# Expert layer of a two-block transformer: 2 MB weight tiles in five slots, second gather and first sum in pieces between the passes

## The reference

```python
def swiglu(t, w_gu, w_down):
    a, g = jnp.split(t @ w_gu, 2, axis=-1)
    return (jax.nn.silu(a) * g) @ w_down

def moe_swiglu(h, w_router, w_gu, w_down):          # 8 experts, D_FF = 2816
    logits = (t @ w_router).astype(jnp.float32)
    top_logit, top_idx = lax.top_k(logits, TOP_K)   # TOP_K = 2
    top_w = jax.nn.softmax(top_logit, axis=-1)
    gate = jnp.einsum('tk,tke->te', top_w, one_hot(top_idx))
    for e in range(N_EXPERTS):
        out = out + gate[:, e:e + 1] * swiglu(t, w_gu[e], w_down[e])
```

## Time and profile before

| | us |
|---|---|
| median of 3 runs | 2047.01 (2045.9 to 2048.48) |
| the profiled execution | 2047.62 |
| its span, first to last instruction | 2045.8 |
| TensorE matmul busy | 1983.7 (97%) |
| DVE busy | 836.6 (41%) |
| ACT busy | 324.9 (16%) |
| bytes by DMA | 485.66 MB, mean 237 GB/s |

### The profile page before, as it was taken

How to read it: one execution, slowest core, us unless ns; L and a number is a source line. 1 busy time by engine, 2 the same in 40 slices (tenths; PEclk the granted TensorE clock), 3 DMA queues, 4 the chain that set the end, 5 groups by cost and what they waited for, 6 DMA issues and landing times.

```text
span 2045.8 us, 31213 instructions
## 1 busy us (share of the span) xinstructions
PE 1983.7 (97%) x13540; PEld 1253.2 (61%) x13540; DVE 836.6 (41%) x1514; ACT 324.9 (16%) x718; POOL 65.6 (3%) x72
## 2 busy tenths in 40 slices
PE   9999999999999999999999989999988999999998
PEld 4888786998458877863333333333333544855997
DVE  4555645456635466561010001110000499444446
ACT  2242111111103411210000000000000232420100
POOL 0000000000000000000000000000000035000000
PEclk9999999999999999998999999999999999999999
DMA  7533543444335244109999999899999732226240
GB/s 311 212 111 137 226 165 139 165 175 161 118 134 196 104 193 198 42 25 419 421 420 420 420 421 396 353 420 420 420 421 421 322 123 108 108 92 248 103 186 21
DMA packets 57036, 485.66 MB, mean 237 GB/s; under 512 B 6544, under 2 KB 6704, under 8 KB 9280
## 3 DMA queue, kind: packets, MB, share of 16 engines
q1 hardware_dynamic: 53424, 464.67, 56.3%
q0 software_dynamic: 3472, 18.95, 2.3%
HBM read 482.54 MB, written 1.05 MB: 236 GB/s over the span
## 4 chain that ended last, share of the span: by engine, by line
PE 87%; DMA 10%; DVE 1%; issue 1%; ACT 1%; SPq 0%; DVEq 0%; ACTq 0%
PE bank L392 46%; PE pair L392 41%; DMA weights<-in_moe_down 8%; DMA weights<-in_moe_up 2%; ACT hT L2945 0%; SPq L3475 0%; DMA const<-in_const 0%; DVE att L1869 0%; DVE h L2260 0%; DVE h L1750 0%; DVE probT L1686 0%; DVE h L1742 0%; DVE att L1870 0%; DVE big L2603 0%; ACT att L3236 0%
## 5 line engine op out<-in xcount | busy, mean ns | idle before, releaser
L392 PE MATMUL bank<-weights,att 128*32 128x512 f32 (+2 forms) x4228 | 392.6, 525 | 15.4 <-issue 13.9
L392 PEld LDWEIGHTS bank<-weights,att 128*32 128x32 f32 (+1 forms) x4228 | 145.6, 110 | 244.2 <-issue 215.3
L392 PE MATMUL pair<-weights,big 128*32 128x512 f32 (+2 forms) x1606 | 232.9, 587 | 24.2 <-DMA weights<-in_moe_down 24.2
L392 PEld LDWEIGHTS pair<-weights,big 128*32 128x32 f32 (+1 forms) x1606 | 90.3, 120 | 153.4 <-issue 149.9
L392 PE MATMUL bank<-hT,weights 128*128 128x128 f32 (+1 forms) x976 | 164.9, 325 | 0.0
L392 PEld LDWEIGHTS bank<-hT,weights 128*128 128x128 f32 x976 | 144.8, 191 | 17.2 <-issue 6.6
L2244 DVE TENSOR_TENSOR big<-head_gain,bank 128x256 f32<-128x256 f32 (+1 forms) x66 | 24.9, 377 | 295.4 <-ACT head_gain L3194 295.4
L392 PE MATMUL pair<-weights,hT 128*128 128x512 f32 (+2 forms) x336 | 137.9, 568 | 1.5 <-ACT hT L2945 1.2
L3194 ACT ACTIVATE head_gain<-bank 128x256 f32<-128x256 f32 (+1 forms) x66 | 23.0, 349 | 550.6 <-PE bank L392 550.6
L392 PEld LDWEIGHTS pair<-weights,hT 128*128 128x128 f32 x336 | 63.3, 190 | 71.5 <-issue 70.0
L392 PE MATMUL pair<-hT,weights 128*128 128x128 f32 (+1 forms) x784 | 105.0, 293 | 0.9 <-ACT hT L2945 0.8
(11 more groups left out here) (478 smaller groups left out, 2422.7 us busy)
## 6 DMA issues: line engine op xcount, KB each, us to landing
weights<-in_moe_up SPq DMA_DIRECT2D x176, 1024.0 KB, 16.7
weights<-in_moe_down SPq DMA_DIRECT2D x88, 1024.0 KB, 18.5
weights<-in_w_in SPq DMA_DIRECT2D x17, 2048.0 KB, 7.5
weights<-in_ffn_up SPq DMA_DIRECT2D x11, 2048.0 KB, 7.3
weights<-in_even_in SPq DMA_DIRECT2D x10, 2048.0 KB, 13.4
weights<-in_mem_wkv SPq DMA_DIRECT2D x8, 2048.0 KB, 7.3
weights<-in_odd_in SPq DMA_DIRECT2D x8, 2048.0 KB, 7.2
norm_par<-in_norms POOLq DMA_DIRECT2D x11, 1024.0 KB, 7.6
```

What stands on the lines that cost most here:

```text
L392: ins = pe.matmul(o, lhsT, rhs, **flags)
```

## The change

What it does, all of it in the way by few tokens:

1. Tiles are whole slots of 2 MB: for each chunk of the up part one tile of each of the four experts, for the down part steps of 4, 4, 4, 4, 4 and 2 row blocks (`FEW_DOWN`). There are 136 tiles in place of 264, five buffers in place of ten. The load of tile i waits for tile i - 5. TensorE makes each pass over the whole chunk at once. The first tile goes to slot `first + 4`, so that the stage ends with the slot ahead of the one with which the even stage begins.
2. SP reads a rank just ahead of the first tile of that expert, and in the second group just ahead of that group's tiles, in place of all eight ahead of the first load.
3. `few_gather(1)` is cut into its eight products, one behind pass 1 of each of the chunks 1 to 8 of group 0; `few_T` is doubled. `few_put(0)` is put behind pass 0 of chunk 0, `few_put(1)` behind pass 1 of chunk 10 of group 0; `put_T` is doubled.
4. `few_sum(0)` is cut into its four pieces, behind pass 1 of the chunks 1, 3, 5 and 7 of group 1. DVE's copies and additions are put in the matching places.
5. On DVE `gated_picks(0)` goes behind `few_gathered(0)`.

The core of the diff:

```diff
-            def few_half(i, first, src):
-                m = i % NHALF
-                if i >= NHALF:
-                    sp.wait_ge(*L.at(f"half{m}_used", i // NHALF))
...
+                    parts = [("moe_up", 4096 * c, 4096) for c in range(HID_CHUNKS)]
+                    parts += [("moe_down", D * sum(FEW_DOWN[:n]), D * nk) for n, nk in enumerate(FEW_DOWN)]
+                    for name, at, width in parts:
+                        for x, r in enumerate((2 * g, 2 * g + 1, 4 + 2 * g, 5 + 2 * g)):
+                            if x not in mine:
+                                mine[x] = sp.value_load(order_i[0:1, r:r + 1], min_val=0, max_val=N_EXPERTS - 1)
...
+                            s = few_slot(first, i)
+                            if taken[s]:
+                                sp.wait_ge(*L.at(f"few{s}_used", taken[s]))
...
+            def few_pass(q, steps, slots, name=None):
+                for last, j, ins in steps:
+                    if last and (q, j) in ((1, 2), (2, 1)):
+                        ins.then_inc(sems(f"few{slots[q - q % 2]}_used"), 1)
+                if name:
+                    end_late(ins, name)
+                if q and name:
+                    slot_owed[0] = f"few{slots[q - q % 2 + 1]}_used"
+                elif q:
+                    ins.then_inc(sems(f"few{slots[q - q % 2 + 1]}_used"), 1)
+
+            def few_up(g, c):
+                slots = [few_tile(), few_tile()]
+                for q in range(PASSES):
+                    if q == 2:
+                        slots += [few_tile(), few_tile()]
+                    name = ("few_up", g, c, q)
+                    o = begin(banks, name, late=True)
+                    few_pass(q, few_up_pass(g, c, q, o, slots), slots, name)
+                    if q == 0 and c:
+                        few_hidden_T(g, c - 1)
+                    if q == 0 and (g, c) == (0, 0):
+                        few_put(0)
+                    if q == 1 and g == 0 and 1 <= c <= KD:
+                        few_gather(1, c - 1)
+                    if q == 1 and (g, c) == (0, PUT_CHUNK):
+                        few_put(1)
+                    if q == 1 and g == 1 and c in SUM_CHUNKS:
+                        few_sum(0, *divmod(SUM_CHUNKS.index(c), 2))
...
                 with pe.Else():
                     few_group(0)
-                    few_gather(1)
-                    few_sum(0)
                     few_group(1)
-                    few_sum(1)
+                    for t in range(NT):
+                        for i in range(2):
+                            few_sum(1, t, i)
...
                 gates()
+                for k in range(KD):
+                    few_gathered(0, k)
                 gated_picks(0)
-                few_gathered(0)
```

More of the change, by code:

```diff
@@ L92, with few_slot, few_uses @@
 C_END = 1256
-def half_uses(m):
-    return len(range(m, FEW_TILES, NHALF))
+def few_slot(first, i):
+    return (first + FEW_FIRST + i) % NSLOT
+def few_uses(first, s):
+    return sum(few_slot(first, i) == s for i in range(FEW_TILES))
 def weight_tiles(k_tiles, widths, group):
@@ L1199, in owner, with few_up_pass @@
                 return j % 2 if q == 1 else q + j // 2
-            def few_up_pass(g, c, q, o, halves, kh):
-                for k in range(KD // 2):
+            def few_up_pass(g, c, q, o, slots):
+                for k in range(KD):
+                    if c == 0 and q == 0:
+                        pe.wait_ge(*emptied(("few_T", g, k)))
                     for j in range(4):
-                        m = halves[owner(q, j)]
-                        tile = weights[:, m // 2, HALF * (m % 2) + 512 * k:HALF * (m % 2) + 512 * k + 512]
+                        tile = weights[:, slots[owner(q, j)], 512 * k:512 * k + 512]
                         out, flow = o[QUAD * j:QUAD * j + QUAD, :], tile
@@ L1210, in few_up_pass @@
                             flow = tile.rearrange("p (a h n) -> p a h n", a=2, h=2)[:, :, j // 2, :]
[L1211 to L1215, removed]
+                        ins = mm(out, few_T[g][k][:, quad_columns(q, j)], flow, start=(k == 0), stop=(k == KD - 1))
@@ L1217, in few_down_pass @@
+                        yield k == KD - 1, j, ins
+            def few_down_pass(q, k0, nk, outs, slots):
                 for i in range(1 if q == 1 else 2):
-                    for k in range(2):
+                    for k in range(nk):
                         for j in range(4):
-                            m = halves[owner(q, j)]
-                            at = HALF * (m % 2) + D * k + 512 * (j // 2 if q == 1 else i)
+                            at = D * k + 512 * (j // 2 if q == 1 else i)
@@ L1229, in few_group @@
-            def few_group(g):
[L1230 to L1235, removed]
-                for c in range(HID_CHUNKS):
[L1237 to L1260, removed]
@@ new lines, in few_down_pass @@
+                                     weights[:, slots[owner(q, j)], at:at + 512],
+                                     start=(k0 + k == 0), stop=(k0 + k == KF - 1))
+                            yield k == nk - 1 and i == (0 if q == 1 else 1), j, ins
+            def few_pass(q, steps, slots, name=None):
[8 more added lines that the diff above has]
+                    ins.then_inc(sems(f"few{slots[q - q % 2 + 1]}_used"), 1)
@@ L1263, in few_group @@
                         [whole[2][:, i, :] for i in range(2)]]
-                for n in range(FEW_STEPS_DOWN):
-                    final = n == FEW_STEPS_DOWN - 1
+                k0 = 0
+                for n, nk in enumerate(FEW_DOWN):
+                    final = k0 + nk == KF
                     if final:
@@ L1268, in few_group @@
                             pe.wait_ge(*emptied(("few_hidT", g, HID_CHUNKS - 1, i)))
-                    halves = [half_tile(), half_tile()]
+                    slots = [few_tile(), few_tile()]
                     for q in range(PASSES):
                         if q == 2:
[L1272 to L1282, removed]
+                            slots += [few_tile(), few_tile()]
+                        few_pass(q, few_down_pass(q, k0, nk, outs[q], slots), slots, ("few_down", g, q) if final else None)
@@ L1283, in few_group @@
                     if n == 0:
                         few_hidden_T(g, HID_CHUNKS - 1)
[L1286 to L1298, removed]
+                    k0 += nk
@@ new lines, in few_sum @@
+            def few_sum(g, t, i):
+                if (t, i) == (0, 0):
+                    pe.wait_ge(*emptied(("few_put", g)))
+                o = begin(banks, ("few_sum", g, i, t), late=True)
+                for q in range(PASSES):
+                    if (t, i) == (0, 0):
+                        pe.wait_ge(*emptied(("few_down", g, q)))
+                    r = slice(64 * i, 64 * i + 64) if q == 1 else slice(0, P)
+                    block = (0, 2, 1)[q]
+                    y = few_y[q][r, 0:512] if q == 1 else few_y[q][:, 512 * i:512 * i + 512]
+                    ins = mm(o[:, :], put_T[g][r, block, t * P:(t + 1) * P], y, start=(q == 0), stop=(q == PASSES - 1))
+                end_late(ins, ("few_sum", g, i, t))
@@ L1349, in moe @@
                     L.seen = seen
-                    for m in range(NHALF):
-                        pe.sem_inc(sems(f"half{m}_used"), half_uses(m))
+                    for s in range(NSLOT):
+                        pe.sem_inc(sems(f"few{s}_used"), few_uses(tiles_used[0], s))
                     pe.sem_inc(sems("banks_filled"), IN_FEW["banks_filled"])
@@ L3436, in load @@
                 s = i % NSLOT
-                if s in halved:
-                    halved.discard(s)
-                    for m in (2 * s, 2 * s + 1):
-                        sp.wait_ge(*L.at(f"half{m}_used", half_uses(m)))
+                if s in lent:
+                    sp.wait_ge(*L.at(f"few{s}_used", lent.pop(s)))
                 into(s, i // NSLOT, src, width)
```

150 lines of the change are left out of this document (81 added, 69 removed).

## The result

The changed kernel takes 2065.52 us (median of 5 runs, 2061.10 to 2069.99) and the kernel before 2047.28 beside it. The ratio is 1.0086, with a 95% interval of 1.0066 to 1.0106. The prediction was 2035, with 2052 at the upper end: wrong in sign and outside of the range. The times of the changed kernel also lie further apart, 9 us from lowest to highest, where those of the one before span 4.

The account below looks back on a forecast made before the run. The expert stage was held bound by its bytes, 659 us at 420 GB/s, plus queue losses. Head, chunks, pairs, steps and ends summed to an end at 1587.3, 11.9 us before 1599.2, giving 2035; range 2022 to 2052.

Parts of the forecast that it names:

- the look-ahead: Up chunks: a loop of 19.1 us fits beside 19.6 of transfer; with 0.15 for scatter, 19.75 per chunk.
- The loop: Up chunks, from a tile's landing to the next landing in its slot: 11.5 us to release, 0.3 to issue, 7.2 to land.
- l: Up chunks: lateness of a tile beyond a lone load's 7.2 us; bites from 0.6, eats the whole gain at 1.2.
- The dry queue: Rival, at the wait for the tile five before: shallow queue runs dry, l of 2 costs 27 us, 2062; chance 0.18.
- the down steps: Down part: passes 0 and 1 take 10.3 us, all three 17.2, with room for a lowered clock; 19.75 per step.
- The scatter: DMA engines do not land together, slowest some 3 us behind the mean; 0.15 us added per chunk.
- The sum in pieces: Group 1 chunks with sum pieces of 2.95 us: 40.7 per two chunks against 39.5, four times 1.2 us.
- The size of the tiles: Whole expert stage: 16 KB pieces move at 428 GB/s in place of 420, 12 us less.
- The head: Stage start: loads begin 4.4 us earlier, lost again as the queue stands 940.5 to 945.8; chunk 1 at 951.7.
- The change of groups: Between groups: TensorE's gather and sum in one piece make a dent costing 10.9 us; pieces were to remove it.
- The ends of the groups: Last down step has 1 MB tiles: pass 2 ends 16.0 us behind its fourth tile's landing, next group's second tile lands at 22.4.

Follow-up runs that it names:

- after: The profiled execution of the changed kernel, 2067.64 us; median of the changed kernel 2065.52 us.
- ten halves: Changed kernel without the large tiles: 1 MB tiles in ten buffers as before, other parts of the change kept; 2035.35 us, ratio 0.9955.
- The transposes' run: Changed kernel with the transposes of the hidden values behind pass 1 in place of pass 0; 2057.12 us, ratio 1.0049.
- without most of pass 1: Changed kernel with seven of eight k steps left out of pass 1 in every up chunk, result wrong; 2046.59 us, one run.
- the reads alone: Kernel before with only the ranks read one by one ahead of each expert's first tile; 2045.04 us, ratio 0.9983.
- the six halves: The 1 MB kernel with all other parts of the change, but six of its ten buffers in use; 2072.77 us, ratio 1.0112.
- eight: The 1 MB kernel with all other parts of the change, but eight of its ten buffers in use; 2037.62 us, ratio 0.9950.
- seven halves: The 1 MB kernel with all other parts of the change, but seven of its ten buffers in use; 2042.81 us, ratio 0.9974.

## Why the prediction was wrong

*The step that failed* is the look-ahead: "It fits, by 0.5 us ... I add 0.15 us per chunk (ends 0 and 1.5)". The ten chunks of group 0 took 20.7 each, 0.95 more than the 19.75 of the forecast. That lies within the ends that the step itself named; the range did not carry them, though 1.35 more on each of 21 chunks and steps is 28 us. The loop itself was priced nearly right, as this timeline of SP's queue and of TensorE in after shows:

```profile
964.37 1.05 SPq L3508 DMA_DIRECT2D weights<-in_moe_up  x2
...
973.38 7.07 PE L401 MATMUL bank<-weights,att 128*32 128x512 f32 x64 [0.91 <-issue]
```

Pass 1 ends at about 964.1, the load is issued at 964.37 (0.3 behind, as priced), and pass 0 starts with its landing at 973.38: 9.0 us after issue, where a lone 2 MB load lands in 7.2. From the landing to the next such issue at 985.42 are 12.0, priced 11.8. So l, the lateness in the flow, was 1.8 here; ten chunks at 19.1 + l = 20.7 give 1.6 on average, if the loop binds in each of them.

What l consists of can be read from the 16 increments of the landing semaphore. Of the load issued at 964.37 eight parts are in 7.20 us later, just as a lone load would be, fifteen 7.51 later and the last 8.92 later. The nine awaited loads from 960 to 1130 have their eighth part on average 7.1 us behind the issue and their last 8.6. So the queue as a whole is not late: one or a few of its 16 parts are, and TensorE can't start before the last.

The dry queue was the second rival, with its break-even at 1.2; rows 7 already had a lone load of 8.4, an l of 1.2. It took the right mechanism and the right place. That its estimate for l of 2, 27 us, is near the 30 that came is in part luck: with the 1.6 measured it gives 13 x 1.0 + 4 x 1.6 = 19, and the rest came in the pairs, the down steps and the ends, which it had at little. What was wrong is the weight that I gave it, 0.18, and the reason against it: "an engine that is ahead there is only made to wait here". That waiting is the loss: while the others stand, their share of the rate is gone. The sign that I had named for it, a share of 0.95 or less all through the up chunks, was too coarse as well: windows of 50 us from 1000 to 1250 have 0.97 to 0.99, and 98.0% in place of 100.8 is the loss.

*The scatter* was read off right as a mean, "some 3 us", but used as if it were an offset, and it is no fixed quantity. From first to last part of a load it is 1.9 us in the middle of the changed kernel's loads from 960 to 1130 and 3.3 with ten halves, and from 1300 to 1480 with ten halves it is 8.4, at 420 GB/s and without loss. My reading is that a deep queue lets the engines drift apart, since each goes on with its own parts, and a shallow one makes those ahead wait, which costs their time. That a load has to be asked for ahead of its turn by more than the lateness of the slowest part fits the dose, but no run has set the one against the other in steps.

*The sum in pieces* was priced at 40.7 us a pair and took 43.8. Its late pass 1 makes a late load, TensorE waits for it, and one thing more comes in that I had priced only for the down part: the clock. Windows of after, columns as in rows 2:

```profile
1384.00:1390.00 6.00, 5.80 (x32) 1.61 (x36) 0.00 (x0) 0.00 (x0) 0.00 (x0) 0.56 0.99 421
...
1394.00:1396.00 2.00, 2.00 (x30) 1.22 (x32) 1.06 (x2) 0.20 (x1) 0.00 (x0) 1.00 0.10 33
```

After waiting 5.04 us, TensorE is granted 0.56 of its clock, mostly the lower of its two levels (1.2 of 2.4 GHz), from 1384 to 1390; pass 0 takes 9.55 in place of 7.07, and the next free tile comes 2.5 later. The load that was awaited had been issued at 1372.48. Fifteen of its 16 parts were in by 1379.66, 7.2 us later, and the last at 1384.11. At 1394 to 1396 the queue is nearly empty for the same reason: of the loads still out, fifteen parts were done by 1394.33 and the last at 1398.77. The release behind the slow pass would have come at 1396.2 even at full clock, too late to fill that gap. So the clock lengthens the loop behind a wait, by 1.7 to 2.5 us; that it brings about the next wait is not shown, and here the next pair had one of 0.9. The pair 1337.02 to 1384.20 took 47.2, and 4.5 of them are the wait for this one part. The transposes' run shows how near to the edge this is: with 1.14 us of slack the pairs are back at 41.0, close to the 40.7 of the forecast.

*The size of the tiles.* 428 GB/s was right for a queue that nothing holds up (19.58 us per chunk without most of pass 1) and was not reached over this kernel's stage. In the same 170 us of the flow the ten halves moved 71.22 MB and the changed kernel 69.42. The estimate worked out from the Trainium skill (DMA: Bandwidth & Descriptors, Why small descriptors are slow) was 0.6% for the doubled pieces; the trace without most of pass 1 has 1.9% at its best, 428 against 420, and for the stretch as a whole 58.44 / 138.0, 423 GB/s, 0.8%. The packets themselves speak for the larger figure: from 1000 to 1100 us one of 16 KB takes 0.611 us in the middle of all, two of 8 KB 0.624 to 0.626, 2% more. The term was of the right size, and out of reach.

*The head.* Right: chunk 1 starts 37.9 us behind the count, predicted 38.7. The reads saved 3.8 (issue 2.21 behind the count in place of 6.02), priced 4.4. That the queue then stands is seen too: 295 GB/s at a share of 0.70 in the window 936 to 946, 3 us lost, where 5.3 were predicted. With ten halves, where the queue doesn't stand, the same 3.8 us bring 2.65 (the run of the reads alone).

*The change of groups.* Right: the dent of 11 us goes. It goes as well without large tiles, for 6 to 8 us, and this part of the change, with the reads, was what was worth having.

*The ends of the groups* were 1.6 and 2.1 us longer than priced, the down steps 0.4 to 0.7 each. There the loop is only 10.3 + 0.3 + 7.2 = 17.8 long, and still a step takes 20.1 and 20.4, and in the run with less of pass 1 up to 21.1. That the scatter does this too is likely, since 2 us of slack are no more than the six halves have, but no run was made on the down part.

*What makes single parts late* was not tested, but the traces point at one thing. In the kernel of ten halves the last part of a load falls behind the eighth in steps and stays there: from 2.2 to 3.7 us at the load landing at 1048.7, from 3.2 to 4.7 at 1147.0, from 3.2 to 4.8 at 1267.7 and from 5.7 to 7.3 at 1469.5. Some 2 to 3 us before each of these landings a packet of the instruction queue (16 KB, 1.0 to 1.1 us each) goes through the DMA engines, at 1045.4, 1144.0, 1264.8 and 1467.3. Such a packet stands shortly before each of the 23 steps of 0.9 us or more in the five kernels whose queue stays full in the flow (before, the reads alone, ten, eight and seven halves). These packets come some 13 us apart, so that chance would put one there for about one step in three; and only about one packet in ten makes a step. So part of the scatter seems to be the program's own instructions being fetched through the same 16 engines; a run that changes the length of the program alone would tell.

## What to carry to other kernels

A stage that is bound by its transfers is worth only as much as its queue is kept full. Before you trade many small buffers for few large ones of the same total, compute for the tightest load how far ahead of its turn it is asked for, from the release and not from the mean depth. If that is no more than the few us by which the last part of a load lands behind the others, price the dry queue as the likeliest case; and carry the ends that you name for a term into the range. Work that frees no buffers goes in pieces between the passes; it cost nothing here as long as that distance was kept.

## What I had not expected of the hardware

- How sharp the edge is: with 1 MB tiles, one buffer less cost 5 us and the next 30 (seven halves 2042.81, six 2072.77).
- A wait of TensorE for a load is paid twice, the second time through the clock: 5.04 us of waiting, then 9.55 in place of 7.07 for the same 32 matmuls.
- A load of 2 MB took 11.6 us in the flow, fifteen of its 16 parts 7.2, as a lone one takes: a single late part held up all the rest.
- Under a full queue the parts of one load land ever further apart, 8.4 us from first to last in the middle of the loads from 1300 to 1480 with ten halves, and the rate stays at 420 GB/s.
